# Fifteen gate blocks moved among the recurrent chain of a decoder block

## The chip, the cores and the metric

One core of one Trainium2 chip runs the whole program. The metric is device time in microseconds. Before the change it is 2598.03 us, the median of three runs (2596.94 to 2599.16).

## The reference, cut to what matters

One layer, one sequence of 512 tokens, width 1024, all float32. A modulation (shift, scale, gate) is computed from a conditioning vector; then:

```
h = rms_norm(x, norm1_gain) * (1 + scale1) + shift1
proj = h @ w_in     # aq ak av | dq dk dv | dz | dbeta dalpha | gate_a gate_b
y_a = sliding_window_attention(qa, ka, va, sinks) @ w_attn_branch
od  = gated_delta_rule(q, k, v, g, beta)          # 8 heads, chunks of 64 tokens
    # t_mat = inverse(eye + a_low); u = t_mat @ v_beta; w = t_mat @ (k_beta * exp(gc))
    # per chunk: v_new = u - w @ state
    #            o = (q * exp(g)) @ state + qk @ v_new
    #            state = state * exp(g_last) + (k * exp(g_last - g))^T @ v_new
od  = rms_norm(od, dn_out_norm) * silu(dz)
y_b = od @ w_dn_branch
mix = (sigmoid(gate_a) * y_a + sigmoid(gate_b) * y_b) @ w_out
x   = x + gate1 * mix
x   = x + gate2 * peer(rms_norm(x, norm2_gain) * (1 + scale2) + shift2, ...)
```

The last line, a mixer over 16384 experts, takes most of the time and is not touched.

## The kernel before, in words

Activations stand transposed: channels on the 128 partitions, tokens along the row. A float32 product with weights is made of three products of rounded halves: each weight slab and each activation is split into a high part (ScalarE rounds) and a low part (VectorE subtracts), and TensorE adds high by high, high by low and low by high. A block is 128 output channels by 512 tokens, 8 chunks of the contraction by 3 products, 24 matmuls of 512 columns. Slabs of two blocks (1 MB) come through the class `Stream`: SyncE loads, `split_hi` on ScalarE, `split_lo` on VectorE, `multiply` on TensorE, with two buffers. A load waits until the low part of the slab before last is made, a high split until the products of the slab before last are done.

Each phase is a block in which every engine has its own program, written out by hand in order. Engines wait for one another by counted semaphores; nothing reorders within an engine, so whatever is queued behind a waiting instruction waits too.

`phase_project` (L428) makes the projections for attention and for the delta rule, with the short convolution on VectorE (`conv`), and lets the attention's steps run among the delta rule's blocks. `ada_after` and `ada_mixed` say behind which block or in which attention step each of 32 chunks of the modulation is summed on TensorE; GpSimd makes the partial sums. `amplitude` (L838) is a chain of 36 small operations on VectorE, `decays` makes g, `sums` (L855) its running sum.

`phase_delta` (L912) is the recurrent stage. It takes four tiles of 128 tokens (two chunks), all 8 heads at once, two groups of four heads (`q`). For each tile: GpSimd copies this tile's k, v and coefficients to fixed places and writes the identity to `inv` and `invT`; ScalarE squares q and k; 32 instructions with a column of ones sum the squares (L992); the coefficients `cf` come from a root and an exponential; TensorE transposes k and v (L1002) and spreads coefficients over partitions (L1008, `spread`); ScalarE scales the transposed k and v (L1106 to L1108, 24 instructions); VectorE forms differences, scaled keys and queries, the decay `E`, and `AT` and `QKT`. The inverse is built in six levels (L1042, L1050, L1051, VectorE L1163, L1196, L1198). Then u and w (L1058, L1059), and for each chunk: w by state (L1072), difference `vnew` (L1210), state product (L1077), output (L1084 and L1085, states by scaled queries and values by scores, turn by turn in one bank), and the states' update on VectorE (L1216), which waits for the output as well. A hardware loop runs tiles 1 to 3. Nothing else uses TensorE in this stage, and the first two slabs of the mixing are loaded during the last tile.

`phase_mix` (L1237) streams 32 slabs: 4 for z (SiLU), then gate A and attention branch in turn (4 and 4), gate B and delta branch in turn (4 and 4), 4 for the output projection, 8 for the queries of the last mixer. `heads(s)` says which heads of the delta rule's output are normed behind slab s: two behind none and one each behind slabs 2 to 9; a head costs an all-ones matmul, a root on ScalarE, and a mean, a reciprocal and two products on VectorE.

## Time and profile before

| | us |
|---|---|
| median of three runs | 2598.03 |
| the profiled execution | 2598.93 |
| its span, first to last instruction | 2597.1 |
| TensorE busy | 2386.9 (92%) |
| VectorE busy | 1749.8 (67%) |
| ScalarE busy | 949.2 (37%) |
| GpSimd busy | 732.8 (28%) |
| mean granted clock of TensorE | 0.944 of full |

The profile's engines are PE (TensorE's matmuls), PEld (its weight loads, beside them), DVE (VectorE), ACT (ScalarE), POOL (GpSimd) and SP (SyncE). A matmul's busy time overlaps its neighbours', so TensorE's rate is read from the distance between starts. PEclk is the clock granted to TensorE as a share of 2.4 GHz; it has two levels, 0.50 and 1.00, and a figure between them is a mean over a stretch.

### The profile page before, as it was taken

How to read it: one execution, taken by the hardware profiler on the slowest of the kernel's cores; microseconds unless marked ns; L12 is line 12 of the kernel's file. 1: busy time of each engine (PE TensorE's matmuls, PEld its weight loads, DVE VectorE, ACT ScalarE, POOL GpSimd, SP SyncE). 2: the span in 40 equal slices, each digit the busy share in tenths (PEclk: the TensorE clock that was granted, in tenths of full speed). 3: DMA queues.
4: the chain of work that ended last, by engine and by line, in shares of the span. 5: the costliest groups of instructions: out<-in, count | busy, mean ns of one | idle time of the engine just before them, and what ended most of it. 6: DMA issues, size and time to landing. Idle time of an engine off the chain costs nothing.

```text
span 2597.1 us, 33865 instructions
## 1 busy us (share of the span) xinstructions
PE 2386.9 (92%) x13069; PEld 2078.5 (80%) x13069; DVE 1749.8 (67%) x3202; ACT 949.2 (37%) x1632; POOL 732.8 (28%) x661
## 2 busy tenths in 40 slices
PE   7898896887778899989899999989999999999998
PEld 2686776877777778768799999988888888888887
DVE  3469883342534374352698899978788887888877
ACT  2335783021120443232455555533333333333332
POOL 0467551010010000000366643343333333333330
PEclk9998997776968899999999999999999999999999
DMA  7333310000001232322333346699989888889984
GB/s 260 107 106 122 114 58 1 1 1 1 0 0 32 81 98 91 120 65 81 118 123 123 128 161 200 213 348 329 316 317 320 313 322 315 324 320 342 324 309 148
DMA packets 214691, 438.39 MB, mean 169 GB/s; under 512 B 22119, under 2 KB 129808, under 8 KB 214288
## 3 DMA queue, kind: packets, MB, share of 16 engines
q1 hardware_dynamic: 166752, 266.52, 30.5%
q0 software_dynamic: 45568, 163.60, 17.5%
q10 hardware_dynamic: 2224, 6.29, 0.6%
q8 instruction: 95, 1.56, 0.2%
q14 instruction: 52, 0.43, 0.0%
HBM read 392.32 MB, written 44.04 MB: 168 GB/s over the span
## 4 chain that ended last, share of the span: by engine, by line
PE 42%; DVE 8%; ACT 1%; issue 1%; DMA 0%; POOL 0%; ACTq 0%; POOLq 0%
PE bank L1823 20%; PE bank L1721 5%; DVE hot_j L2039 5%; PE bank L1809 3%; PE bank L1807 3%; PE bank L1808 3%; PE bank L1727 2%; PE bank L1691 2%; DVE hot_i L2034 2%; ACT ha L1871 1%; PE bank L1701 1%; PE bank L1743 1%; DVE o_nat L2103 0%; DMA ug<-in_peer_u_dram,gidx 0%; DVE o_nat L2102 0%
## 5 line engine op out<-in xcount | busy, mean ns | idle before, releaser
L1653 POOL TENSOR_TENSOR ua_lo<-ua,ua_hi 128x512 fp32r<-128x512 f32 x128 | 202.1, 1584 | 560.4 <-ACT ua L1858 560.2
L1823 PE MATMUL bank<-vt_hi,wg_hi 128*128 128x512 f32 x768 | 248.1, 404 | 5.2 <-DVE wg_lo L2093 4.9
L1646 POOL DMA_INDIRECT ug<-in_peer_u_dram,gidx x128 | 146.1, 1141 | 329.3 <-DVE ug L2049 326.3
L1823 PE MATMUL bank<-vt_lo,wg_hi 128*128 128x512 f32 x768 | 239.0, 392 | 0.0
L1823 PE MATMUL bank<-vt_hi,wg_lo 128*128 128x512 f32 x768 | 238.3, 391 | 0.0
L2075 DVE TENSOR_TENSOR vt_lo<-vt_raw,vt_hi 128x1024 fp32r<-128x1024 f32 x128 | 156.1, 1219 | 92.4 <-ACT vt_hi L1945 92.4
L1675 POOL DMA_INDIRECT vg<-in_peer_v_dram,gidx x128 | 131.2, 1025 | 237.9 <-DVE g_acc L2064 225.6
L1721 PE MATMUL bank<-h_hi,ua_hi 128*128 128x384 f32 x512 | 184.1, 360 | 12.3 <-ACT ha L1871 12.1
L1807 PE MATMUL bank<-h_hi,uT_hi 128*128 128x384 f32 x512 | 176.7, 345 | 0.0
L1721 PE MATMUL bank<-h_lo,ua_hi 128*128 128x384 f32 x512 | 174.0, 340 | 0.0
L1809 PE MATMUL bank<-h_hi,uT_lo 128*128 128x384 f32 x512 | 171.8, 335 | 0.0
L1823 PEld LDWEIGHTS bank<-vt_hi,wg_hi 128*128 128x128 f32 x768 | 135.3, 189 | 45.2 <-issue 24.3
L1945 ACT ACTIVATE vt_hi<-vt_raw 128x1024 fp32r<-128x1024 f32 x128 | 135.1, 1056 | 98.6 <-PE bank L1823 98.6
L1808 PE MATMUL bank<-h_lo,uT_hi 128*128 128x384 f32 x512 | 171.1, 334 | 0.0
L1823 PEld LDWEIGHTS bank<-vt_hi,wg_lo 128*128 128x128 f32 x768 | 144.8, 188 | 31.9
L1823 PEld LDWEIGHTS bank<-vt_lo,wg_hi 128*128 128x128 f32 x768 | 144.7, 188 | 31.8
L1956 ACT ACTIVATE wg_hi<-wt 128x384 fp32r<-128x384 f32 x128 | 67.3, 526 | 276.2 <-DVE wt L2088 273.0
L388 DVE TENSOR_TENSOR mx_lo<-mx_raw,mx_hi 128x2048 fp32r<-128x2048 f32 x32 | 73.3, 2292 | 137.1 <-ACT mx_hi L384 137.1
L2064 DVE SCALAR_TENSOR_TENSOR g_acc<-vg,g_hw,g_acc 128x1024 f32<-128x1024 f32 x127 | 162.5, 1280 | 1.4 <-DMA vg<-in_peer_v_dram,gidx 0.3
L2049 DVE SCALAR_TENSOR_TENSOR ug<-ug,h2n 128x1024 f32<-128x1024 f32 x128 | 155.5, 1217 | 3.2 <-DMA ug<-in_peer_u_dram,gidx 3.2
L2039 DVE TENSOR_SCALAR hot_j<-iota,picked,picked 128x128 f32<-128x128 f32 x384 | 145.7, 439 | 0.0
L1847 ACT ACTIVATE uT_hi<-bank 128x512 fp32r<-128x512 f32 x128 | 76.1, 594 | 189.5 <-PE bank L1691 189.5
(417 smaller groups left out, 5945.4 us busy)
## 6 DMA issues: line engine op xcount, KB each, us to landing
u_raw<-in_peer_u_dram SPq DMA_DIRECT2D x128, 512.0 KB
vt_raw<-in_peer_v_dram SPq DMA_DIRECT2D x128, 512.0 KB
gates<-g_stage SPq DMA_DIRECT2D x12, 2048.0 KB, 8.9
gate<-gates SPq DMA_DIRECT2D x32, 768.0 KB, 7.5
pj_raw<-in_w_in_dram SPq DMA_DIRECT2D x16, 1024.0 KB, 5.2
ada_w<-in_w_ada_dram POOLq DMA_DIRECT2D x32, 512.0 KB, 4.5
mx_raw<-in_w_in_dram SPq DMA_DIRECT2D x12, 1024.0 KB, 5.2
hid_keep<-ha POOLq DMA_DIRECT2D x64, 192.0 KB, 2.7
```

Source lines behind the costliest of these rows:

```text
L1646: nc.gpsimd.indirect_dma_start(ug[s % RING][:], None, u_rows, bass.IndirectOffsetOnAxis(m.gidx[:, s:s + 1].bitcast(U32), 0)).then_inc(s_ug ...
L1653: nc.gpsimd.tensor_tensor(ua_lo[b % 2][:, 4 * q:4 * q + 4, :], ua[b % 2][:, 4 * q:4 * q + 4, :], ua_hi[b % 2][:, 4 * q:4 * q + 4, :].bitca ...
L1721: last = pe.matmul(o, ua_hi[b % 2][:, k, :], (m.h2_lo if low else m.h2_hi)[:, k, P:], start=(n == 0), stop=False)
L1807: pe.matmul(o, uT_hi[f % 2][:, k, :], m.h2_hi[:, k, P:], start=(k == 0), stop=False)
L1808: pe.matmul(o, uT_hi[f % 2][:, k, :], m.h2_lo[:, k, P:], start=False, stop=False)
L1809: last = pe.matmul(o, uT_lo[f % 2][:, k, :], m.h2_hi[:, k, P:], start=False, stop=(k == KC - 1))
L1823: ins = pe.matmul(y_bank[t][q][:], w[n % 2][:, tok], v[n % 2][:, 512 * q:512 * q + 512], start=(first and i == 0), stop=(last and i == 2))
L1945: nc.scalar.activation(v_hi[n % 2][:], v_raw[n % 4][:], ACT.Copy).then_inc(x["vhi"], 1)
L2039: ins = v.tensor_scalar(B[n % 4][:, t, :], m.iota[:], jT[:, col], gT[:, col], ALU.is_equal, ALU.mult)
L2049: v.scalar_tensor_tensor(ug[s % RING][:], ug[s % RING][:], 1.0, m.h2n[:], ALU.mult, ALU.mult, accum_out=h_raw[:, s:s + 1]).then_inc(x["dot ...
L2064: ins = v.scalar_tensor_tensor(acc[:], vg[s % RING][:], h_w[:, s:s + 1], acc[:], ALU.mult, ALU.add)
L2075: v.tensor_tensor(v_lo[n % 2][:], v_raw[n % 4][:], v_hi[n % 2][:].bitcast(F32), ALU.subtract)\
```

## The change

Recurrent stage. The hardware loop is written out, so tiles are addressed directly, GpSimd's copies go, and so does the start value of the inverse. Fifteen blocks, the 8 of z and 7 of gate A, are computed in this stage: `load` on SyncE, `high` and `gate` on ScalarE, `low` on VectorE, and `fill(n)` on TensorE, which issues the next n of 360 matmuls at written places, with a pair of banks of their own. The gates of A go to DRAM tile by tile (`keep`) and are read back by the mixing. The weights of block 16 are split here as well. The first level of the inverse no longer multiplies by the identity: TensorE transposes `AT`, and VectorE masks both `AT` (with the new constant `above`) and its transpose. Values are scaled on VectorE (8 instructions), keys on ScalarE (16). The squares of the next tile wait only for the last `vnew`. States by scaled queries stand before the state product, values by scores come once for both chunks, behind everything, and the states' update no longer waits for the output.

Mixing. The order is: block 16 (the last of gate A), one gate slab of B, four of the attention branch, three gate slabs of B, four of the delta branch, then as before; 24 slabs instead of 32. Heads are normed behind slabs 0 to 5 as 1, 1, 2, 1, 1, 2.

Projection. Small moves of order, in the diff's first part.

```diff
-    ada_after = {i: [c] for c, i in enumerate((6, 8, 9, 10, 11, 12, 14, 15, 16, 17, 18, 19, 20))}
+    ada_after = {i: [c] for c, i in enumerate((6, 8, 9, 10, 12, 13, 18, 19, 20))}
@@ project, PE and DVE
-                if b == 1:        # transposes of g; on DVE sums()
+                if b == 2:
@@ project, ACT
+                if s == 0:
+                    split(2)
                 for half in range(2):
                     copy_out(2 * s + half)
-                split(s + 2)
+                if s:
+                    split(s + 2)
@@ and square(2), square(3) ahead of v_hi; on DVE amplitude() behind split_lo(5)
...
@@ delta, PE
+            def fill(n):
+                for i in range(place[0], place[0] + n):
+                    f, j = divmod(i, 3 * KC)
+                    k, term = divmod(j, 3)
+                    if j == 0:
+                        pe.wait_ge(f_lo, f + 1)
+                        if f >= 2:
+                            pe.wait_ge(f_read, f - 1)
+                    last = pe.matmul(F_BANK[f % 2][:], (hi, hi, lo)[term][f % 2][:, k, :],
+                                     (m.h_hi, m.h_lo, m.h_hi)[term][:, k, :], start=(j == 0), stop=(j == 3 * KC - 1))
+                    if j == 3 * KC - 1:
+                        last.then_inc(f_ready, 1)
+                place[0] += n
@@ fills in a tile, in order of the program
+                if not first:
+                    fill(24)                       # ahead of the ones-matmuls
+                fill(36 if first else 12)          # behind the spread of g
+                fill(0 if last_tile else 4)        # between the two score products
+                    if l < 4:                      # in each level, behind its first product
+                        fill(16 if l == 0 else 0 if last_tile else 3)
+                fill(8 if last_tile else 10)       # behind u and w
+                    fill(6)                        # in each chunk, ahead of the state product
+                    if c == 0:
+                        fill(0 if last_tile else 9)
@@ delta, PE, chunk
+                    for h in range(DNH):
+                        at = P * (h % G) + CHUNK * c
+                        pe.matmul(bank[h // G][:, at:at + CHUNK], S[:, h, :], qg[:, h, rows],
+                                  start=(c == 0 and h % G == 0), stop=False)
+                for h in range(DNH):               # once a tile, behind the second chunk
+                    last = pe.matmul(bank[h // G][:, P * (h % G):P * (h % G) + P], vnew[:, h, :], E[:, h, :],
+                                     start=False, stop=(h % G == G - 1))
@@ delta, ACT
+            def high(f):
+                act.wait_ge(f_loaded[f % 2], 16 * (f // 2 + 1))
+                if f >= 2:
+                    act.wait_ge(f_ready, f - 1)
+                nc.scalar.activation(hi[f % 2][:], raw[f % 2][:], ACT.Copy).then_inc(f_hi, 1)
@@ ACT per tile: squares, copies out of the tile before, gate(b0-1), high(b0+1), root, exp, scaled keys,
@@   exp of the differences, gate(b0), high(b0+2), gate(b0+1), high(b0+3), u and w, gate(b0+2), high(b0+4)
@@ DVE per tile: low(b0+1) first, low(b0+2) behind E, low(b0+3) behind the levels, low(b0+4) behind the
@@   first update of the states; in the first tile low(0) and low(1) behind the differences
@@ delta, DVE
+                    if l == 0:
+                        dve.wait_ge(z["Pm"], t * 12 + 2)
+                        for q in range(2):
+                            hs = slice(G * q, G * q + G)
+                            v.tensor_tensor(inv[:, hs, :], eye, prod[:, hs, :], ALU.subtract)
+                            v.tensor_tensor(invT[:, hs, :], eye, invT[:, hs, :], ALU.subtract).then_inc(z["D"], 1)
+                        continue
-                    dve.wait_ge(z["o"], t * 2 + (cc + 1))
@@ mix
-    A, B, OUT, WQ, N = 4, 12, 20, 24, 32
+    GATES, A, B, OUT, WQ, N = (0, 5, 6, 7), 1, 8, 12, 16, 24
-        return range(max(s - 2, 0), min(s - 1, DNH)) if s < B else range(0)
+        return ((0,), (1,), (2, 3), (4,), (5,), (6, 7))[s] if s < 6 else ()
+            for k in range(KC):
+                pe.matmul(bank[6][:], m.rest_hi[:, k, :], m.h_hi[:, k, :], start=(k == 0), stop=False)
+                pe.matmul(bank[6][:], m.rest_hi[:, k, :], m.h_lo[:, k, :], start=False, stop=False)
+                last = pe.matmul(bank[6][:], m.rest_lo[:, k, :], m.h_hi[:, k, :], start=False, stop=(k == KC - 1))
...
```

## Rows read from the trace of the kernel before

**Rows 1.** Stages: us; busy us (instructions) of PE, PEld, DVE, ACT, POOL; clock; DMA.
```profile
91.40:408.20 316.80, 279.44 (x1576) 229.57 (x1576) 238.83 (x356) 185.67 (x355) 187.09 (x167) 0.95 0.33 104
408.20:852.80 444.60, 354.62 (x2328) 340.65 (x2328) 170.62 (x366) 63.24 (x160) 28.08 (x33) 0.77 0.02 5
852.80:1084.90 232.10, 227.74 (x976) 185.07 (x976) 119.34 (x98) 87.78 (x94) 0.00 (x0) 0.98 0.28 91
```
**Rows 2.** Waits of the recurrent stage: who for whom: us in total, times, longest.
```profile
PE bank L992 <- ACT dn_sq L1096: 21.3, 4, 7.7
PE bank L1008 <- ACT vb L1108: 18.0, 4, 4.8
...
DVE states L1216 <- PE bank L1085: 78.3, 8, 11.0
```
**Rows 3.** Timeline (start, us), second chunk of tile 0: output and update.
```profile
513.93 0.69 PE L1084 MATMUL bank<-qg,states 128*128 128x64 f32 x2
...
521.13 2.15 DVE L1216 SCALAR_TENSOR_TENSOR states<-states,ee,bank 128x128 f32<-128x128 f32 x8 [10.96 <-PE bank L1085]
```
**Rows 4.** Short stretches: output matmuls of tile 0, transposes and scaled copies of tile 2.
```profile
494.00:500.00 6.00, 6.00 (x29) 5.78 (x29) 0.00 (x0) 0.00 (x0) 0.00 (x0) 0.50 0.00 0
647.00:648.00 1.00, 1.00 (x8) 1.00 (x8) 0.49 (x4) 0.00 (x0) 0.00 (x0) 0.68 0.00 0
650.00:654.00 4.00, 0.00 (x0) 0.00 (x0) 1.90 (x8) 4.00 (x17) 0.00 (x0) 1.00 0.00 0
```
**Rows 5.** Timeline, heads of tiles 1 and 2.
```profile
525.57 6.99 PE L992 MATMUL bank<-ones,dn_sq 128*128 128x1 f32 x32 [4.55 <-ACT dn_sq L1096]
534.07 0.17 DVE L1142 TENSOR_SCALAR dn_ms<-bank 128x16 f32<-128x16 f32 x1 [10.79 <-PE bank L997]
...
636.28 6.99 PE L992 MATMUL bank<-ones,dn_sq 128*128 128x1 f32 x32 [4.54 <-ACT dn_sq L1096]
646.15 1.77 PE L1002 MATMUL bank<-ident,vTs 128*128 128x128 f32 x8
```
**Rows 6.** Timeline, tile 0: first products of levels 0, 1 and 5, and u.
```profile
444.49 1.13 PE L1042 MATMUL bank<-inv,AT 128*128 128x128 f32 x8 [1.60 <-DVE AT L1163]
...
452.32 1.06 PE L1042 MATMUL bank<-inv,AT 128*128 128x128 f32 x8
...
476.75 1.06 PE L1042 MATMUL bank<-inv,AT 128*128 128x128 f32 x8
...
481.23 0.45 PE L1058 MATMUL bank<-vb,invT 128*128 128x128 f32 x2
```
**Rows 7.** Timeline of ScalarE, mixing: the first three blocks of z read.
```profile
865.48 0.60 ACT L1335 ACTIVATE z<-bank 128x512 f32<-128x512 f32 x1 [6.60 <-PE bank L423]
870.92 0.60 ACT L1335 ACTIVATE z<-bank 128x512 f32<-128x512 f32 x1 [4.84 <-PE bank L423]
...
876.36 0.60 ACT L1335 ACTIVATE z<-bank 128x512 f32<-128x512 f32 x1 [2.00 <-PE bank L423]
```
**Rows 8.** Timeline of TensorE, the first matmul of the mixing.
```profile
857.12 0.80 PE L421 MATMUL bank<-h_hi,mx_hi 128*128 128x512 f32 x1 [6.86 <-DVE mx_lo L388]
```
**Rows 9.** Timeline of VectorE, mixing: one head, from its mean to its last product.
```profile
920.89 0.68 DVE L1387 TENSOR_SCALAR od_rs<-bank 128x512 f32<-128x512 f32 x1
...
926.45 0.69 DVE L1394 TENSOR_TENSOR z<-od_rs,dn 128x512 f32<-128x512 f32 x1
```
**Rows 10.** Groups of the recurrent stage: count, busy us, mean ns, idle before.
```profile
L1177 DVE SCALAR_TENSOR_TENSOR E<-diff,dn_r,cum 128x128 f32<-128x128 f32 x32 | 12.8, 470 | 0.0
L979 POOL TENSOR_TENSOR Es<-E,strict 128x512 f32<-128x512 f32 x8 | 10.3, 1288 | 117.0 <-DVE E L1177 117.0
```
**Rows 11.** Waits of TensorE in the projection.
```profile
PE bank L655 <- DVE g L835: 9.1, 1, 9.1
...
PE bank L562 <- DVE pj_lo L388: 3.5, 1, 3.5
PE bank L582 <- ACT at_sq L682: 3.2, 1, 3.2
```

More of the change, by code:

```diff
@@ L125, in constants @@
     m.level = m.small("level", [P, 6, P])
+    m.above = m.small("above", [P, P])
     m.amask = m.small("amask", [P, 2, 2 * P])
@@ L992, in body @@
                     pe.matmul(bank[0][:, j:j + 1], sq[:, j, :], m.ones[:, 0:1], start=True, stop=True)
-                pe.wait_ge(z["stage"], t * 2 + 1)
-                pe.matmul(bank[0][:, 24:32], sel[:], gs[:], start=True, stop=True)
+                pe.matmul(bank[0][:, 24:32], sel[:], gs, start=True, stop=True)
                 for c in range(2):
@@ L1020, in body @@
                         pe.wait_ge(z["kb"], t * 2 + (h // G + 1))
-                    last = pe.matmul(bank[2 + h // G][:, P * (h % G):P * (h % G) + P], kTs[:, h, :], kb[:, h, :],
+                    last = pe.matmul(bank[2 + h // G][:, P * (h % G):P * (h % G) + P], kT[:, h, :], kb[:, h, :],
                                      start=True, stop=True)
@@ L1079, in body @@
                     last.then_inc(z["st"], 1)
-                    if c == 1:
-                        pe.wait_ge(z["oe"], t * 2 + 1)
-                    for h in range(DNH):
-                        cols = slice(CHUNK * h, CHUNK * h + CHUNK)
-                        pe.matmul(bank[4][:, cols], S[:, h, :], qg[:, h, rows], start=True, stop=False)
-                        last = pe.matmul(bank[4][:, cols], vnew[:, h, :], QKT[:, h, rows], start=False, stop=True)
-                    last.then_inc(z["o"], 1)
+                    if c == 0:
+                        fill(0 if last_tile else 9)
@@ new lines, in gate @@
+            def gate(f):
+                act.wait_ge(f_ready, f + 1)
+                if f < DNH:
+                    nc.scalar.activation(m.z[:, f, :], F_BANK[f % 2][:], ACT.Silu).then_inc(f_read, 1)
+                else:
+                    if f > DNH:
+                        act.wait_ge(f_sig, 16 * (f - DNH))
+                    nc.scalar.activation(sig[:], F_BANK[f % 2][:], ACT.Sigmoid).then_inc(f_read, 1)
+            for t in range(NT):
+                tok = slice(P * t, P * t + P)
+                b0 = 4 * t
+                if t:
+                    act.wait_ge(z["vn"], t * 2)
+                nc.scalar.activation(sq[:, DNH:, :], m.dn[:, DNH:2 * DNH, tok], ACT.Square)
+                nc.scalar.activation(sq[:, 0:DNH, :], m.dn[:, 0:DNH, tok], ACT.Square).then_inc(z["sq"], 1)
+                if t:
+                    act.wait_ge(z["o"], t)
+                    nc.scalar.activation(m.carry[:], m.ones[:, 0:1], ACT.Copy)
+                    for q in range(2):
+                        last = nc.scalar.activation(m.dn[:, G * q:G * q + G, P * (t - 1):P * t],
+                                                    bank[q][:].rearrange("p (h n) -> p h n", h=G), ACT.Copy)
+                    last.then_inc(z["oe"], 1)
+                    gate(b0 - 1)
+                    high(b0 + 1)
@@ L1173, in body @@
                     by(q, qg, m.dn[:, G * q:G * q + G, tok], 6, z["qg"])
+                dve.wait_ge(z["bq1"], t + 1)
+                for q in range(2):
+                    by(q, q1, m.dn[:, G * q:G * q + G, tok], 0, z["q1"])
                 for q in range(2):
@@ L1218, in body @@
                     last.then_inc(z["S"], 1)
-            loop(dve, body, c, 4)
+                    if cc == 0 and t < NT - 1:
+                        low(b0 + 4)
 def mix_slabs(a):
@@ L1228, in mix_slabs @@
     w_q = a["peer_w_q"].rearrange("o (k p) n -> p (o k) n", p=P)
-    slabs = [w_in[:, :, COL_Z + SLAB * i:COL_Z + SLAB * i + SLAB] for i in range(DNW // SLAB)]
-    for gate, branch in (((w_in, COL_GA), (w_a, 0)), ((w_in, COL_GB), (w_b, 0))):
-        for i in range(D // SLAB):
-            slabs += [w[:, :, base + SLAB * i:base + SLAB * i + SLAB] for w, base in (gate, branch)]
+    part = lambda w, base: [w[:, :, base + SLAB * i:base + SLAB * i + SLAB] for i in range(D // SLAB)]
+    gates = part(w_in, COL_GB)
+    slabs = gates[:1] + part(w_a, 0) + gates[1:] + part(w_b, 0)
     slabs += [w_o[:, :, SLAB * i:SLAB * i + SLAB] for i in range(D // SLAB)]
@@ L1328, in _ @@
             split(1)
+            for k in range(KC):
+                nc.scalar.activation(y_hi[:, k, :], at[:, k, :], ACT.Copy).then_inc(z["ahi"], 1)
+            act.wait_ge(z["rest"], 1)
+            nc.scalar.activation(sig_a[3][:, 1, :], bank[6][:], ACT.Sigmoid).then_inc(z["rest_sig"], 1)
             square(0)
@@ L1331, in _ @@
             for s in range(OUT):
-                if s < A:
-                    for half in range(2):
-                        act.wait_ge(st.ready, 2 * s + half + 1)
-                        nc.scalar.activation(m.z[:, 2 * s + half, :], bank[2 * (s % 2) + half][:], ACT.Silu)\
-                            .then_inc(st.read, 1)
-                elif s % 2 == 0:
-                    gate(s, sig_a if s < B else sig_b)
+                if s in GATES:
+                    gate(s)
                 if s == OUT - 1:
@@ L1420, in _ @@
                         low_mix(k)
-                if s > A and s % 2:
+                if s not in GATES:
                     branch(s)
-                if s == B:
+                if s + 2 < OUT + 1:
+                    st.split_lo(dve, s % 2, s + 2)
+                for n in heads(s):
+                    mean(n)
+                    normed(n)
+                if s == 6:
                     for k in range(KC):
```

303 lines of the change are left out of this document (169 added, 134 removed).

## The prediction

> **What bounds the kernel now.** The stage table comes first [rows 1]: projection 316.8 us, the recurrent stage (delta rule) 444.6 us, the mixing up to the output projection 232.1 us, the rest 1512 us. Only the first three change. TensorE is busy in 279 of 317, 355 of 445 and 228 of 232 us, but in the recurrent stage its granted clock averages 0.77 against 0.95 and 0.98 beside it. So the mixing is bound by TensorE's work alone, and the recurrent stage by a chain of engines that hand on to each other, with half-clock matmuls in it. The waits of the stage say the same from both sides [rows 2]: TensorE waits 21.3 us for the squares at the head of each tile and 18.0 us for ScalarE's scaled copies, VectorE 78.3 us for the last output matmul before it may update the states. The timeline shows that last one: the state product is out at about 513.9, then the output's 32 instructions run until 521.1, and only then comes the update of 2.15 us, though it needs the state product alone [rows 3]. The clock rows tell what is slow in there: 0.50 in the output matmuls [rows 4], and the ones-matmuls take the time of that clock too (below). A tile's period, from ones to ones, is 636.28 - 525.57 = 110.7 us [rows 5].
>
> **Units.** An fp32 matmul is two instructions here. One level of the inverse is 48 instructions in (476.75 - 452.32) / 4 = 6.11 us [rows 6], a wait of some 0.7 among them; they follow each other every 0.111 us at full clock. The 32 ones-matmuls and six more take from 525.57 to 534.07, less a little latency 8.2 us at half clock [rows 5], 0.217 each, so 0.107 to 0.111 at full clock. A gate block (24 matmuls of 512 columns) takes 876.36 - 870.92 = 5.44 us [rows 7], 0.227 each.
>
> **Mixing: what is removed.** 20 slabs of two blocks stand before the output projection; 12 and one single block are left. Eight slabs by 10.88 us are 87.0 us gone. The single block comes first. Today TensorE waits 6.9 us there and starts at 857.12, 4.3 us into the stage [rows 8]; the new block needs no split and fills that hole, but runs mostly at half clock as the first matmuls do now (the first half is read at 865.5, 8.3 us for 24 matmuls). It ends about 8.0 us in; the first block ended its cold part (2.9 us above 5.44) and the 4.3 us start before, so 0.8 us is lost net. Heads: one costs VectorE 926.45 + 0.69 - 920.89 = 6.2 us, a low split 2.2 [rows 9], two products of a branch 1.4. I lay them out in the new order (heads 1, 1, 2, 1, 1, 2 behind slabs 0 to 5; blocks of 5.44, a head's own squares on TensorE 0.9). VectorE is through with head 1 at 41 us, 3 at 59, 4 at 69, 5 at 79, 7 at 96, and the eight low parts of y at 103; slabs 3, 5 and 6 find their weights split within 0 us of need, and TensorE comes to the first delta branch slab (8) at 102.4. So a stall of 0.6. Mixing gain: 87.0 - 0.8 - 0.6 = 85.6 us. Its bounds: the 79 us that remain if the new single block is fully exposed and the heads stall 1.5 us, and 87.
>
> **Recurrent stage, a middle tile at full clock.** Zero is the end of the second chunk's state matmuls. TensorE: values by scores for all heads in 16 instructions 1.8; fill of 24, 5.4 (to 7.2); ones and sums 4.1 (11.3). Beside it the update of the states (2.2), ScalarE's two copies out, a gate (0.6, a table load of 1.3 with it) and a split (1.1) end by 7.6, and the squares were made before, since they now wait for nothing but the chunk's difference; so the 21.3 us wait goes. Coefficients 2.8 us later as now, 14.1; 16 transposes and 16 spread instructions to 14.9; fill 12 to 17.6. ScalarE's scaled copies are 16 now instead of 24, a quarter us each (17 in 4.0 us): 4.0 plus latency, 18.5. VectorE takes the other eight (2.1) and the differences (some 2.2), 18.5 as well [rows 4]. TensorE stalls 0.9 instead of 4.5 [rows 2]. Three spreads (5.4), first product 1.8, fill 4 of 0.9, second 1.8: 28.4. VectorE: last scaled query 25.3, E 3.2 (28.5, 0.4 us pitch from [rows 10]), GpSimd's mask 1.3 (29.8), AT at 30.4 and 31.0. The first level now is 8 transposes, 16 fills hidden behind VectorE's two score products, two masks, two products and four differences of about 0.6 each: 31.0 + 5.3 = 36.3. From its first product to the next level's that is 5.9 us where it is 452.32 - 444.49 = 7.8 now [rows 6], so only 2 us go. Levels 1 to 3 take 6.1 + 0.7 for three fills (a fill between product and product is added, since the wait of 0.48 behind it stays) less 0.4 at the first, level 4 6.1, the last with the two products behind it 8.1 (481.23 - 476.75 and 3.6) [rows 6]: 70.2. ScalarE's copies 2.1, under ten fills: 72.5. Each chunk is 16 + 16 + 6 fills + 16 instructions, 1.8 + 1.8 + 1.4 + 1.8 = 6.8, with VectorE's difference (1.3) under the fills, and 2.4 for the update between them, under nine fills: 72.5 + 6.8 + 2.4 + 6.8 = **88.5 us**, against 110.7.
>
> Where the cover could go: the splits of VectorE (1.2 each) stand in front of the coefficients, behind E, behind the last level and behind the update. Each is done 1 to 4 us before what TensorE wants next; if one is late it costs its own 1.2. SP's eighteen steps (loads of 512 KB, keeps of 256 KB behind them) always wait for an event of an earlier group; a keep has some 10 us before its tile is written again.
>
> **First and last tile.** At the first, the squares start at 408.3 and not 411.4, ones end 418.6 (half clock), G at 424.4. Then TensorE must wait for VectorE's eight copies, the differences and two splits: 427.9. 36 fills take 8.2 and about 2.5 for a cold start: 438.6; from there as above (88.5 - 18.5): 508.6, where it is 513.9 now. The last tile has 24 fills fewer, but only those on the chain count (3 x 0.7): 86.5. Then 3.2 for the last output and copies. Stage: 100.4 + 177.0 + 86.5 + 3.2 = 367.1 against 444.6, so 77.5 us gone at full clock.
>
> **Clock.** Ones-matmuls, chunk matmuls of 64 rows or columns: these ran at 0.50 [rows 4, 5]. Now warm fills stand between them. Bounds: nothing, and all of it at half clock, that is 6.8 x 2 + 2.0 + 1.8 + 5.4 + 4.1 + 3.6 = 30.5 us more per tile, four times 122, less some 14 of stalls that it covers, 108. I take 3 us for the head of each of three tiles (one drop in the ones, paid in the transposes) and 1 us per recurrence, 13 us, near the lower end, because of all rows at half clock none has 512-column matmuls close before it. Stage gain: 64.5 us.
>
> A rule that speaks against this: between 647 and 648 the clock rises to full (0.68 in the mean), and what runs there is the second half of the transposes, from 646.15 on [rows 4, 5]. The Trainium skill (TensorE: Matmul & The Clock Gate, Part 4: PE-mode transpose) says that full clock doesn't engage for transpose-mode matmuls. By that rule 24 transposes per tile would be paid at 0.217 instead of 0.111, 10 us over four tiles; by the row nothing. I go by the row.
>
> **Projection.** Three waits [rows 11]. The 3.5 us one: VectorE's 36 small operations (7.2 us) stood before the split of slab 2; moved away, TensorE no longer waits there, but the split now precedes the copy out, and the wait for that copy of 1.0 grows by 1.9: net -1.8 (it starts at 94.1, ends 99.7, before 101.5). The moved operations fall into VectorE's idle 8.9 us. The 3.2 us for the squares shrinks by v_hi's 2.0. The 9.1 us for g: one more block (5.4) goes in front, but the next needs a bank that the first convolution frees, so 2.4; the scans then stand later on VectorE, by up to 2.7 for the first softmax. Four more modulation chunks go among the attention steps: GpSimd needs 5.8 us for one, a step lasts 11.5, hidden. Sum -5, between -8 and -1. The constant `above` costs three operations of 0.25 us under the loads.
>
> **Sum.** The profiled execution lasted 2598.93 us (span 2597.1), 0.9 over the median of 2598.03. 2598.9 - 85.6 - 64.5 - 5 = 2443.8; the median may be 0.9 lower. I forecast **2444 us**.
>
> **Rivals.**
> - No clock loss: 13 us less, 2431. For it: a TensorE almost without gaps. Against: the 38 ones and sums in a row. 0.13.
> - The clock stays half in head and recurrence (the 108 instead of 13): 2539. For it: all rows of these matmuls at 0.50. Against: 60 fills in those stretches. 0.10.
> - Heads late: if each of eight roots needs its table load (1.3) on VectorE's path, slab 8 waits 10 us: 2454. Now it is loaded ahead in all rows. 0.12.
> - The transposes go unclocked, the rule above: 2454, 0.04.
> - The fills cost in the recurrent stage what the edits there save: stage at 444 as now, only 85.6 + 5 gained, 2508. 0.05.
> - Slower: the fills run neither warm nor hidden. 360 matmuls at 0.453 are 163 us in line; the other edits of the stage give back about 57 (three operations of the first level 21, GpSimd's copies 9, 128 output instructions 27). Stage +106, others -91: 2614. It decides from a growth of the stage by 91 us. Against: TensorE was idle 90 us there. 0.02.
> - The projection gains nothing: 2449, 0.04.
> - Forecast, 2430 to 2458: 0.50.
>
> The range 2422 to 2480 leaves out the three far cases (0.17). About 0.2% (5 us) can be told from no change. Faster 0.975, same 0.005, slower 0.02.
>
> **What would show it.** The stage table: recurrent stage about 380 us at a clock of 0.95 or more, mixing 146 to 147 until the output projection, projection 312. TensorE's wait for the squares gone, the one for the scaled copies about 1 us a tile, VectorE's 78.3 us gone, period 89 to 94. Wrong if the period is over 98, if ones or chunk matmuls show 0.50 over whole tiles, if TensorE waits in the fills for a low split, or if slab 8 of the mixing waits for over 3 us.

## The result, and the profile after

The changed kernel takes 2448.14 us (median of 4 runs, 2446.27 to 2452.55) where the kernel before takes 2597.61 (2596.94 to 2599.16): 0.9425 of its time, 95% interval 0.9411 to 0.944. The forecast was 2444. The profiled span is 2444.4 us against 2597.1. The stage table, cut at the same events as before (start and end; us; busy us and instructions of PE, PEld, DVE, ACT, POOL; granted clock; DMA share; GB/s):

```profile
91.00:409.30 318.30, 280.89 (x1576) 230.17 (x1576) 252.31 (x355) 185.59 (x355) 189.14 (x166) 0.94 0.33 103
409.30:789.20 379.90, 350.24 (x2464) 320.40 (x2464) 200.02 (x418) 82.63 (x159) 14.80 (x9) 0.94 0.11 33
789.20:933.40 144.20, 143.52 (x616) 115.48 (x616) 100.80 (x89) 55.20 (x64) 0.00 (x0) 1.00 0.31 101
```

Beside [rows 1]: the recurrent stage went from 444.6 to 379.9 us (-64.7; forecast -64.5), the mixing from 232.1 to 144.2 (-87.9; forecast -85.6), and the projection ends 1.1 us later (it starts 0.4 earlier, so it is 1.5 longer) where -5 was forecast. What follows takes 1511.0 us instead of 1512.2. The four together are -152.7, the whole difference of the spans. In the recurrent stage TensorE issues 136 instructions more (360 of the gates, minus those removed), and the granted clock is 0.94 instead of 0.77.

The waits of that stage (who for whom: us in total, times, longest):

```profile
DVE states L1315 <- PE bank L1115: 32.0, 8, 4.0
PE bank L1071 <- DVE AT L1250: 10.5, 8, 2.7
...
PE bank L1019 <- ACT dn_sq L1152: 4.5, 1, 4.5
```

The wait for the squares, 21.3 us at four tiles in [rows 2], is left at the first tile alone (4.5); the 18.0 us for the scaled copies are gone altogether; VectorE waits 32.0 us for the state product instead of 78.3 for the output. What each of these is worth alone isn't shown: the experiments take back only the update's place (e6) and the first level (e3). The timeline of tile 2 shows what stands there now (start, us, instructions):

```profile
603.52 2.05 PE L1121 MATMUL bank<-E,vnew 128*128 128x128 f32 x16
603.62 2.15 DVE L1315 SCALAR_TENSOR_TENSOR states<-states,ee,bank 128x128 f32<-128x128 f32 x8 [3.99 <-PE bank L1115]
610.89 4.86 PE L1019 MATMUL bank<-ones,dn_sq 128*128 128x1 f32 x32
616.90 3.38 PE L1028 MATMUL bank<-ident,dn 128*128 128x128 f32 x16
636.55 0.66 PE L1071 MATMUL bank<-ident,AT 128*128 128x128 f32 x4 [1.75 <-DVE AT L1250]
643.01 2.27 PE L1073 MATMUL bank<-inv,AT 128*128 128x128 f32 x16 [0.81 <-DVE invT L1292]
```

The update starts with the output product (603.62 beside 603.52) and no longer behind the output's 32 instructions, as it did in [rows 3]. From one output product to the next are 92.85 us here; the four stand at 512.15, 603.52, 696.37 and 785.68. Two stretches of the same tile show the clock, chunks and then ones and transposes:

```profile
589.00:603.00 14.00, 14.00 (x97) 11.91 (x97) 5.64 (x13) 2.01 (x2) 0.00 (x0) 1.00 0.15 39
613.00:619.00 6.00, 6.00 (x30) 6.00 (x30) 0.68 (x5) 1.68 (x3) 0.00 (x0) 0.50 0.01 3
```

In the mixing TensorE starts at full clock and waits once, before the first delta-branch slab:

```profile
789.24 0.47 PE L1387 MATMUL bank<-h_hi,fl_hi 128*128 128x512 f32 x1 [1.51 <-PEq L953]
889.78 0.50 PE L426 MATMUL bank<-y_hi,mx_hi 128*128 128x512 f32 x1 [0.64 <-DVE y_lo L1542]
```

The waits of TensorE in the projection have changed names and not their sum:

```profile
PE bank L608 <- DVE sd L804: 15.8, 4, 10.9
PE bank L619 <- ACT sc L707: 14.5, 11, 4.3
PE bank L567 <- ACT kn L680: 2.9, 1, 2.9
PE bank L587 <- ACT at_sq L687: 1.3, 1, 1.3
```

### The profile page after: what moved, and what is told of

Same layout as the page of the kernel before. It is cut to its first block, busy times and chain, and to the rows that moved or that the text cites. A ratio compares the mean times of both kernels' runs of the same rounds, so it can differ in the third digit from the quotient of the medians.

```text
span 2444.4 us, 33257 instructions
## 1 busy us (share of the span) xinstructions
PE 2299.5 (94%) x12845; PEld 1989.1 (81%) x12845; DVE 1774.4 (73%) x3248; ACT 935.5 (38%) x1601; POOL 723.1 (30%) x637
## 4 chain that ended last, share of the span: by engine, by line
PE 45%; DVE 8%; ACT 2%; issue 1%; POOL 0%; ACTq 0%; DVEq 0%
PE bank L1929 22%; PE bank L1827 5%; DVE hot_j L2145 5%; PE bank L1915 4%; PE bank L1913 4%; PE bank L1914 4%; PE bank L1833 3%; PE bank L1797 2%; DVE hot_i L2140 2%; ACT ha L1977 1%; PE bank L1807 1%; PE bank L1849 1%; DVE o_nat L2209 0%; DVE o_nat L2208 0%; PE bank L1897 0%
## 5 line engine op out<-in xcount | busy, mean ns | idle before, releaser
L2181 DVE TENSOR_TENSOR vt_lo<-vt_raw,vt_hi 128x1024 fp32r<-128x1024 f32 x128 | 156.5, 1223 | 92.5 <-ACT vt_hi L2051 92.5
L2150 DVE TENSOR_TENSOR uT_lo<-bank,uT_hi 128x512 fp32r<-128x512 f32 x128 | 88.3, 690 | 81.9 <-ACT uT_hi L1953 81.9
```

What stands on the lines that cost most here:

```text
L2181: v.tensor_tensor(v_lo[n % 2][:], v_raw[n % 4][:], v_hi[n % 2][:].bitcast(F32), ALU.subtract)\
```

## The experiments

All are edits of the changed kernel. "Against it" is the ratio less 0.9425, times 2598 us; an interval of a ratio is 3 to 6.5 us to either side, that of the changed kernel 3.7. The intervals of e6, e7, e8, e10 and e11 lie apart from the changed kernel's; those of e1, e2, e3, e4, e5, e9 and e12 touch or overlap it, and what is said of these rests on their traces.

| run | median us (range) | ratio [95%] | against it, us |
|---|---|---|---|
| e1 bare fills | 2441.68 (2440.44 to 2444.28) | 0.9396 [0.9379, 0.9414] | -7.5 |
| e2 chunks bare | 2454.97 (2454.54 to 2457.16) | 0.9449 [0.9431, 0.9466] | +6.2 |
| e3 level 0 by products | 2459.09 (2454.5 to 2464.28) | 0.9458 [0.9433, 0.9483] | +8.6 |
| e4 projection undone | 2447.52 (2442.66 to 2450.3) | 0.9421 [0.9408, 0.9434] | -1.0 |
| e5 modulation undone | 2444.71 (2443.07 to 2448.0) | 0.9415 [0.9402, 0.9428] | -2.6 |
| e6 output ahead of update | 2462.71 (2461.98 to 2467.3) | 0.9482 [0.9463, 0.9501] | +14.8 |
| e7 heads late | 2464.83 (2462.67 to 2469.4) | 0.9492 [0.9477, 0.9506] | +17.4 |
| e8 fills redealt | 2433.71 (2433.21 to 2434.48) | 0.9371 [0.9357, 0.9385] | -14.0 |
| e9 scans behind softmax | 2446.18 (2443.01 to 2450.25) | 0.9419 [0.9406, 0.9432] | -1.6 |
| e10 = e8 + e5 | 2431.86 (2428.56 to 2437.03) | 0.9363 [0.935, 0.9375] | -16.1 |
| e11 = e10 + e9 | 2426.80 (2421.76 to 2431.42) | 0.9346 [0.9333, 0.9358] | -20.5 |
| e12 sums early | 2442.22 (2437.74 to 2446.84) | 0.9401 [0.9388, 0.9414] | -6.2 |

**What the fills cost (e1).** Of each gate block only the first and the last matmul are issued.

```diff
+                    if 0 < j < 3 * KC - 1:
+                        continue
                     last = pe.matmul(F_BANK[f % 2][:], ...
```

> The changed kernel, with 22 of the 24 matmuls of each of the fifteen moved blocks left out (330 of 360, 75 us of TensorE at full clock); the loads, splits, gates and waits stay. Theory (the fills lie mostly under other engines' work and hold the clock at 1.00): at full clock a middle tile would lose only the exposed fills, some 8 of 22 us, but the ones-matmuls and the chunk matmuls fall back to 0.50 and cost about 18 us a tile more; the recurrent stage stays near 380 us (370 to 400), the kernel within -10 to +20 us of the changed one. Rival (the fills are a load on TensorE's path, the clock doesn't depend on them): the stage loses 30 to 75 us and the kernel with it, clock still over 0.9.

330 matmuls of 0.227 us, 75 us of TensorE's work, are gone, and 7.5 us with them. Timeline of TensorE, the second chunk of tile 1 and the head behind it:

```profile
586.08 3.67 PE L1107 MATMUL bank<-states,wT 128*64 128x128 f32 x16 [2.25 <-DVE states L1317]
589.68 3.68 PE L1112 MATMUL bank<-qg,states 128*128 128x64 f32 x16
...
593.82 3.78 PE L1117 MATMUL bank<-vnew,kdec 64*128 64x128 f32 x16
597.53 3.78 PE L1123 MATMUL bank<-E,vnew 128*128 128x128 f32 x16
...
602.63 4.72 PE L1021 MATMUL bank<-ones,dn_sq 128*128 128x1 f32 x32 [0.63 <-issue]
```

Sixteen instructions take 3.7 us and not 2.0: half clock, which with the fills was full. The four groups cost 7 us more, and idle stretches of 1.7 to 3.2 us come back elsewhere, as the first row shows one. The periods, output product to output product, are 91.4, 92.2 and 92.2 us beside 91.4, 92.85 and 89.3 with the fills. So in the middle tiles the 20 us of 88 fills are paid by two things. From 597.53 to 689.70 in e1 TensorE is busy 76.7 of 92.2 us at a mean clock of 0.83; from 603.52 to 696.37 in the changed kernel 87.7 of 92.85 us, at 0.96. Its busy time fell by 11 us where 20 of work are gone, so some 9 are the clock that the fills hold, and idle time grew by 10. The theory's bounds for stage and kernel held, its terms less well: it had put the clock at 18 us a tile. What is left is in the first tile: 89.9 us from its ones (416.27) to its last output product (506.14), where it is 100.6 with the fills.

**Where the fills stand (e2, e8).** e2 takes all fills out of levels 1 to 3 and the chunks and puts them in front of the chunks (24 for 10) and into the first level (32 for 16). e8 keeps three in each chunk, takes those between the products of levels 1 to 3 away, puts eight where TensorE waits for AT, behind the score products, and the others behind the spread of g (4 more), into the first level (6 more) and behind the first state product (1 more). Its diff, without the last tile's counts:

```diff
-                fill(36 if first else 12)
+                fill(40 if first else 16)
...
+                fill(8)
-                fill(0 if last_tile else 4)
...
-                        fill(16 if l == 0 else 0 if last_tile else 3)
+                        fill((18 if last_tile else 22) if l == 0 else 0)
...
-                    fill(6)
+                    fill(0 if last_tile else 3)
```

> The changed kernel with the same 360 fills, but none among the two chunks of a tile and none in levels 1 to 3: they stand behind the first product of level 0 (32) and behind u and w (24). Theory (fills among the chunk matmuls keep the clock up there): the chunk matmuls show 0.50 again, some 5 to 11 us a tile, the kernel is 20 to 45 us slower than the changed one. Rival (what precedes is warm enough, the place is indifferent): the chunks stay at 1.00 and only the balance of exposed fills changes, 0 to +6 us.

> The changed kernel with its 360 fills dealt otherwise: in a middle tile 24 ahead of the ones, 16 behind the spread of g, 8 behind the second score product, 22 in level 0, none in levels 1 to 3, 10 behind u and w, 3 in each chunk, 10 behind the first state product. Theory (a fill is free where TensorE waits and costs 0.227 us elsewhere; some 17 fills a tile move from exposed to covered places): -2 to -4.5 us a tile, the kernel 8 to 17 us faster, clock as now. Rival (three fills a chunk are too few to hold the clock): the chunks show 0.50, 10 us or more slower.

e2, TensorE at the second chunk of tile 1 and the first level of tile 2:

```profile
602.60 3.14 PE L1105 MATMUL bank<-states,wT 128*64 128x128 f32 x16 [2.25 <-DVE states L1312]
605.67 2.43 PE L1110 MATMUL bank<-qg,states 128*128 128x64 f32 x16
...
642.92 0.66 PE L1071 MATMUL bank<-ident,AT 128*128 128x128 f32 x4 [1.75 <-DVE AT L1247]
...
653.56 1.95 PE L1073 MATMUL bank<-inv,AT 128*128 128x128 f32 x16
```

The chunks lost 1.6 us to the clock (3.14 + 2.43 for 1.96 + 2.00) and took 15.5 us in all where they took 16.8 with fills; with the 24 fills ahead of them the clock needed few inside. The time went into the first level, where 32 fills make 10.6 us of 6.5, and into the stretch ahead of the chunks. The balance of tile 2, from output product to output product (96.4 us beside 92.85), is +4.2 there, -2.3 in the other levels, +3.2 ahead of the chunks and -1.4 in the chunks. The 6.2 us lie by the rival's 0 to 6; the theory, a loss of clock in the chunks, asked 20 to 45 and falls. But the chunks didn't stay at 1.00, as the rival had it: they ran at 0.89 in the mean. e8 turns that reading round:

```profile
602.07 2.05 PE L1121 MATMUL bank<-E,vnew 128*128 128x128 f32 x16
634.25 0.66 PE L1071 MATMUL bank<-ident,AT 128*128 128x128 f32 x4 [0.83 <-DVE AT L1250]
641.10 1.95 PE L1073 MATMUL bank<-inv,AT 128*128 128x128 f32 x16
```

Periods fall to 90.6, 88.9 and 84.2 us, and from the first ones to the rest block it is 365.4 us instead of 377.6. Of the 4.0 us of the tile shown, 2.3 are levels 1 to 5, mostly the fills between products (0.7 a level, as that step of the prediction had it), 1.2 the chunks (15.6 us for 16.8), and 0.8 the way to AT (32.2 us for 33.0). The first level became 0.4 longer. The way to AT holds eight fills more (1.8 us) and is shorter all the same: TensorE waits 0.83 us for AT and not 1.75, and the ones run at full clock (3.63 us for 4.86). The theory's 8 to 17 holds.

**The first level (e3).** Products with a staged identity instead of transposes and masks.

```diff
-                                last = pe.transpose(o, AT[:, h, :], m.ident[:])
+                            last = pe.matmul(o, AT[:, h, :], inv[:, h, :], start=True, stop=True)
```

> The changed kernel with the first level of the inverse as before: identity written by GpSimd at the tile's start, product with it, two products more. Theory (this level is VectorE's chain plus TensorE's 48 instructions, and the fills stand in it): 3.3 us a tile later, +8 to +14 us for the kernel. Rival (the level is hidden behind the 16 fills and the differences of VectorE): within 2.5 us of the changed kernel.

```profile
644.21 2.38 PE L1074 MATMUL bank<-inv,AT 128*128 128x128 f32 x16 [1.82 <-DVE AT L1250]
...
653.66 1.06 PE L1074 MATMUL bank<-inv,AT 128*128 128x128 f32 x8
```

9.45 us from first product to next level, 6.46 with the masks: 3.0 a tile, 12 in four, and +8.6 by the ratio, 11 by the medians. As the theory had it; the rival, a hidden level, falls by the trace. The four runs are two pairs, 2454.5 and 2455.2, 2463.0 and 2464.3. The trace is of the slower pair, and from the first ones to the rest block it takes 394.1 us instead of 377.6, 4.5 more than the level explains.

**Output ahead of the update (e6).** Each chunk's share of the output is computed behind its state product, in front of what VectorE waits for.

```diff
                     last.then_inc(z["st"], 1)
+                    for h in range(DNH):
+                        last = pe.matmul(bank[h // G][:, at:at + CHUNK], vnew[rows, h, :], E[rows, h, rows], ...
+                    last.then_inc(z["o"], 1)
...
                     dve.wait_ge(z["st"], t * 2 + (cc + 1))
+                    dve.wait_ge(z["o"], t * 2 + (cc + 1))
```

> The changed kernel with the output's second product once per chunk (64 columns, 64 rows) straight behind the state product, and the states' update waiting for it, as before the change. Theory (the order costs its 16 instructions at full clock in the first chunk; in the second the fill of 24 covers it): +1.8 us a tile, +5 to +9 us. Rival (these narrow matmuls pull the clock down, which is what cost 7 us a chunk before): the clock falls below 0.9 in the chunks and the kernel is 20 us or more slower.

VectorE's wait and the start of the rest block:

```profile
DVE states L1317 <- PE bank L1120: 46.9, 8, 6.1
```
```profile
803.58 0.76 PE L1389 MATMUL bank<-h_hi,fl_hi 128*128 128x512 f32 x1 [2.59 <-PEq L953]
```

The wait grew from 32.0 to 46.9 us, 1.9 for each of eight chunks, and the rest block starts 14.3 us later than the 789.24 of the changed kernel. It also starts at half clock (0.76 us for its first matmul), which it doesn't there. The 14.8 us lie between the theory's 5 to 9 and the rival's 20; the share of the first chunk alone, 1.9 a tile in TensorE's own order, would be 8. The trace shows most of the other half. In tiles 1 and 2 it is 12.8 us from the first chunk's start to the second's, where the changed kernel takes 9.6: 1.9 for the 16 instructions, and 1.3 since most of the nine fills behind them run at half clock:

```profile
696.20 0.63 PE L1002 MATMUL bank<-h_lo,fl_hi 128*128 128x512 f32 x1
...
699.23 1.96 PE L1105 MATMUL bank<-states,wT 128*64 128x128 f32 x16
```

The nine take 3.6 us from 695.61 and not 2.3, at a clock of 0.66 between 693.6 and 698.4. That is the rival's mechanism, at 1.3 us a tile and not at the 7 a chunk that it named. In the first and the last tile this distance is 11.4 us; in the last the clock falls in the second chunk instead (0.81 from 790 to 799).

**Heads (e7).** One head behind each of the slabs 0 to 7, as in the kernel before.

```diff
-            return ((0,), (1,), (2, 3), (4,), (5,), (6, 7))[s] if s < 6 else ()
+            return (s,) if s < 8 else ()
```

> The changed kernel with one head normed behind each of slabs 0 to 7 of the mixing instead of 1, 1, 2, 1, 1, 2 behind slabs 0 to 5, and the split of the normed heads behind slab 7. Theory (the first delta branch slab then waits for the last head and eight splits on VectorE): TensorE waits about 15 us ahead of slab 8, +11 to +17 us. Rival (the heads are hidden anyway): within 2.5 us.

```profile
904.38 0.80 PE L426 MATMUL bank<-y_hi,mx_hi 128*128 128x512 f32 x1 [14.93 <-DVE y_lo L1542]
```

14.9 us of wait instead of 0.64, and a clock of 0.62 from 904 to 912. The head's place is worth what the layout of the order said.

**The projection (e4, e5, e9, e12).** e4 puts all its edits back; e5 only the groups of the modulation on GpSimd; e12 only the place of the sums; e9 leaves that place and moves the scans behind the first softmax.

In e4 and e5, ahead of the modulation's chunks; in e4 and e12, at the transposes and at the sums:

```diff
-    ada_after = {i: [c] for c, i in enumerate((6, 8, 9, 10, 12, 13, 18, 19, 20))}
+    ada_after = {i: [c] for c, i in enumerate((6, 8, 9, 10, 11, 12, 14, 15, 16, 17, 18, 19, 20))}
...
-                if b == 2:
+                if b == 1:
```

In e4 alone, also the order of v's high part and of the squares, and the place of VectorE's 36 small operations; in e9 alone the last two lines:

```diff
-                if s == 0:
-                    split(2)
                 for half in range(2):
                     copy_out(2 * s + half)
-                if s:
-                    split(s + 2)
+                split(s + 2)
...
             st.split_lo(dve, 1, 5)
-            amplitude()
...
                     soft(at_score[b])
+                if b == 2:
+                    scans()
```

> The changed kernel with every edit of the projection undone (modulation chunks, transposes of g, order of split and copy, squares, amplitude). Theory from the two traces (the stage ends 1.1 us later after the change, 409.3 against 408.2): the edits bring nothing, the kernel is 0 to 3 us faster than the changed one. Rival (my forecast): they bring 5 us, the kernel is 1 to 8 us slower.

> The changed kernel with only the modulation chunks dealt as before (13 ahead of the attention, 19 in its steps). Theory (GpSimd's work and VectorE's small operations stretch one another: g ends 14 us earlier while GpSimd waits, but four chunks more among the attention steps slow VectorE, which bounds there): g takes 14 us again as before, the attention steps are faster, together within -6 to +2 us of the changed kernel. Rival (GpSimd is indifferent): VectorE's operations keep their times and the kernel its time within 2 us.

> The changed kernel with one thing moved: the two scans and the addition over the decays (5.3 us of VectorE in the trace of the changed kernel, 204.5 to 209.8, ahead of the first softmax) are issued behind the first softmax instead of ahead of it; the copy out of PSUM stays ahead. In the changed kernel TensorE waits 10.9 us at 213.1 for that softmax. Theory (the first softmax is on the path and VectorE has room later): that wait falls from 10.9 to about 5.6, and 3 to 5 us of it reach the end: 2443 to 2445. Rival (from 200 us on VectorE's own queue, busy 46 of 50 us, sets the pace, so the order of its work is of no account): the wait falls but the next ones grow by as much, 2447 to 2449, no change. Worse than 2450 would say that the transposes of the decays now hold TensorE up.

> The changed kernel with one thing undone: the transposes of the decays and their sums stand again behind the second block of the mixed-layer projection and not behind the third. Theory of the prediction (that move took 2.4 us off the path): 2450 to 2451. Rival (the wait for the decays had been over anyway, since they are ready at 188 us in the changed kernel and no longer at 202, so the place is of no account): 2447 to 2449. If the later place is what put the sums ahead of the first softmax, the undone version is faster: 2443 to 2446.

VectorE in the changed kernel, ahead of the first softmax (its last step at 212.92 releases TensorE's `scores` at 213.14, the 10.9 us wait):

```profile
203.81 0.67 DVE L866 COPY gT<-bank 8x512 f32<-8x512 f32 x1
204.52 3.08 DVE L868 TENSOR_TENSOR_SCAN run<-keep,gT 8x512 f32<-8x512 f32 x1
207.63 1.10 DVE L869 TENSOR_TENSOR_SCAN off<-keep,run 8x32 f32<-8x32 f32 x1
208.77 1.10 DVE L872 TENSOR_TENSOR run<-run,off 8x384 f32<-8x384 f32 x1
209.80 1.64 DVE L798 SCALAR_TENSOR_TENSOR sc<-bank,qrs,amask 128x256 f32<-128x256 f32 x4
```

With the sums one block earlier, e12: VectorE, and TensorE's first `scores` and first ones-matmul.

```profile
190.72 0.67 DVE L866 COPY gT<-bank 8x512 f32<-8x512 f32 x1
191.43 1.21 DVE L868 TENSOR_TENSOR_SCAN run<-keep,gT 8x512 f32<-8x512 f32 x1
...
193.48 2.27 DVE L393 TENSOR_TENSOR pj_lo<-pj_raw,pj_hi 128x2048 fp32r<-128x2048 f32 x1
...
198.68 1.65 DVE L798 SCALAR_TENSOR_TENSOR sc<-bank,qrs,amask 128x256 f32<-128x256 f32 x4
```
```profile
203.65 2.08 PE L608 MATMUL bank<-kn,aq 64*128 64x256 f32 x8 [4.81 <-DVE sd L804]
...
400.26 6.96 PE L1019 MATMUL bank<-ones,dn_sq 128*128 128x1 f32 x32 [4.51 <-ACT dn_sq L1152]
```

The first softmax starts at 198.7 and not 209.8, and the ones at 400.26 and not 411.60: 11 us in this execution, of which its later stages gave 6 back (1661.5 us from the rest block on, instead of 1655.2), and 6 in the medians. The intervals of e12 and of the changed kernel still touch (0.9414 and 0.9411).

Not all of the 11 us are the edit's. The last v_hi products of a block that stands ahead of the moved instructions in both, in the changed kernel and in e12:

```profile
173.33 1.16 PE L578 MATMUL bank<-v_hi,h_hi 128*128 128x272 f32 x8
```
```profile
169.85 1.16 PE L578 MATMUL bank<-v_hi,h_hi 128*128 128x272 f32 x8
```

e12 is 3.5 us early there already, 0.4 from the start of the stage and 3.1 by the clock: between 165 and 175 us it was 1.00, in the changed kernel 0.59 and 0.73, with the same instructions in the same order. This drop, behind the squares of attention's q (`at_sq`), stands in the traces of e1, e2, e3, e6, e7, e8 and e9 too; e12's was spared it, so how much of the 6 us in the medians is the place isn't shown. The other 7.6 us lie between the first convolution and the first softmax, 21.6 us in the changed kernel (188.18 to 209.80) and 14.0 in e12. The sums stand in front of that softmax in both. In e12 VectorE makes them while GpSimd is idle, in 2.8 us with their copy and not 6.0 (3.2); they fill the 2.5 us that VectorE otherwise waits for ScalarE's high part of the slab; and the low part behind takes 2.27 us and not 4.10 (1.8):

```profile
196.78 4.10 DVE L393 TENSOR_TENSOR pj_lo<-pj_raw,pj_hi 128x2048 fp32r<-128x2048 f32 x1 [2.50 <-ACT pj_hi L675]
```

That the later place harms, the third reading in e12's expectation, is what fits; the prediction's gain of 2.4 from the move is out.

How far such a difference can be read: the changed kernel and those with its projection (e1, e2, e3, e6, e7, e8) start the ones between 411.6 and 416.3. So e4 (411.0) and e9 (410.5) can't be told from it by their traces, nor by their ratios, and e4's equal time says what the stage table says: the projection's edits brought nothing that can be measured. e5 (407.8) starts them 3.8 us early, of which 3.1 are there before g is made, nearly all by the same clock (1.00 from 165 to 175), as in e10 and e11, which deal the modulation as e5 does. Its mechanism is as its theory had it: g takes 14 us again beside a busy GpSimd, and TensorE waits 3.4 us for it. In e9 the wait for the softmax fell from 10.9 to 5.8, as the theory had it, and too little of it reached the end to be told from none. The scans moved behind bring the first softmax 5.3 us nearer to the first convolution (16.35 us), moved ahead 7.6; where the rest of the difference between e9 and e12 comes from, beyond the 3.1 us of clock, is open.

**Together (e10, e11).**

> The redealt kernel (2433.7) with the modulation groups among the projection's slabs as in the kernel before. Alone on the changed kernel that return brought 2448.1 to 2444.7, with ScalarE's and VectorE's small operations beside GpSimd's work at other places. Theory (the two add, since they act in different stages): 2430 to 2431. Rival (the 3.4 us were the phase in which the recurrent stage meets the clock, not the projection): 2433 to 2435 here.

> The redealt kernel with the modulation groups as before the change and the two scans behind the first softmax. Theory (all three add): 2425 to 2428. Rival (VectorE's queue sets the pace of the projection's second half): as the redealt kernel with the modulation groups alone, 2430 to 2434.

e10 can't be told from e8 (0.9363 and 0.9371, intervals overlapping). e11 is the fastest version measured, 2426.80 us, 0.9346 of the kernel before and outside the interval of the changed kernel; that it adds to e10 isn't certain (0.9363 [0.935, 0.9375]). e8 with the sums early was not run.

## Why the prediction was right, and where it was not

**Mixing, -85.6 forecast, -87.9 measured.** Eight slabs less, and a stall of 0.6 before slab 8: 0.64, with the place of the heads confirmed by e7. The term that was off is the single block: 8.0 us "mostly at half clock" against 5.5 at full clock (0.47 us for its first matmul, where [rows 8] has 0.80), and that is 2.5 us better than forecast. The stretch before it is one of dense work with an idle of 1.5 us; in [rows 8] TensorE had been idle for 6.9. e6, with 2.6 us idle, starts the block at half clock.

**Recurrent stage, -64.5 forecast, -64.7 measured.** First tile, from the stage's start to the output product: 100.4 plus 1 for the clock forecast, 102.9 measured (409.30 to 512.15). Middle tiles: 88.5 plus 4 for the clock, so 92.5; measured 91.4 and 92.85. Last tile: 86.5 plus 4; measured 89.3. The end, 3.2 forecast, is 3.5. So the stage's agreement to 0.2 us is partly luck: errors of up to 1.5 us cancel. The prediction's own terms up to the end of the levels add up to 70.5 and not to its 70.2. Inside a tile: ones at 7.2 forecast, 7.4 measured; the first transposes of AT at 30.4 plus 3 for the head's clock, measured 33.0; first level 5.9 forecast, 6.46 measured, since TensorE still waits 0.67 between its two halves and 0.8 at its end; chunks 16.0 forecast, 16.8 measured, at full clock, so the 1 us a recurrence put down to the clock wasn't lost to it, and the instructions took 0.8 more than their sum. The clock step held in kind: full in the chunks (1.00), and one drop in the ones, paid in the transposes (4.86 and 3.38 us for what takes 3.6 and 1.9 at full clock, 2.7 us). Half clock in the recurrence, the rival of 2539, is what e1 shows without fills, though only in part (0.84 from the first ones to the rest block, 0.95 with them): its stage isn't longer, since the fills' own time is gone with it. The rival in which the fills cost what the edits save falls with the stage's 64.7 us.

**The transposes.** In [rows 4, 5] the granted clock rose while transposes ran. In e4 all 16 transposes of k and v of a tile, one instruction each, ran at full clock, behind ones at full clock:

```profile
612.48 1.94 PE L1025 MATMUL bank<-ident,dn 128*128 128x128 f32 x16
```

0.11 us each. The rule of the Trainium skill (TensorE: Matmul & The Clock Gate, Part 4: PE-mode transpose) that full clock doesn't engage for them does not hold here; no loss of 10 us stands anywhere. The 1.4 us that they lost in the tile of the changed kernel shown above came with the clock that fell in the ones ahead of them.

**Projection, -5 forecast, +1.1 measured.** The failed step is "one more block (5.4) goes in front ... so 2.4; the scans then stand later on VectorE, by up to 2.7". The other waits went as forecast: 3.5 gone with kn's grown from 1.0 to 2.9, the squares' from 3.2 to 1.3. The wait for g went whole, since g is ready at 188.3 and not 202.2, but the sums then stand at 203.8 to 209.8, 6.0 us in front of the first softmax, and TensorE waits 10.9 us there instead of 9.1 for g. The place was priced at 2.7 us, which is what copy, scans and addition take in the kernel before (208.15 to 210.82), with GpSimd idle. In the changed kernel they take 6.0 beside GpSimd, the low part ahead of them 4.10 instead of 2.27, and VectorE idles 2.5 ahead of that: 7.6 us by the traces of e12 and the changed kernel. How much of it reaches the end isn't settled: 6.2 by e12's ratio, with touching intervals and 3.5 of the 11 us of its trace's lead there before the place is reached. The prediction counted GpSimd's work among the attention steps as "hidden", from GpSimd's own time alone, and put nothing on VectorE for it. That g would come 14 us early was missed too: with four modulation groups fewer among the slabs GpSimd is idle while VectorE works on g, and VectorE's small operations take their bare time (last section).

## What to carry to other kernels

Independent matmuls dealt into a dependent chain are paid for by idle time and by the clock that they hold; look in a trace for what each place waits, and deal no more there than that, since between one product and the product behind it every fill costs its own length (0.7 us for three, in e8). When a wait of the fast engine goes, look at what its releaser has queued in front of the next thing wanted, and beside which engine it will run: the 9 us wait for g went, and one of 11 for the first softmax came. Lay moved work out in order on the engine that carries it: for the heads, where this was done, the forecast wait was within 0.1 us of the measured one, and for the sums, where it wasn't, the forecast was several us off.

## What the runs showed of the hardware

A small operation of VectorE with two inputs in SBUF can take fourteen times its length beside GpSimd. The same polynomial step in the kernel before, with what GpSimd did, and in the changed kernel, with GpSimd idle from 183.4 to 195.1:

```profile
187.72 2.62 DVE L831 TENSOR_TENSOR g<-g,dn_t 128x32 f32<-128x32 f32 x1
190.37 1.31 DVE L832 TENSOR_SCALAR g<-g 128x32 f32<-128x32 f32 x1
```
```profile
187.42 0.92 POOL L512 DMA_DIRECT2D ada_w<-in_w_ada_dram  x1 [0.30 <-POOL ada_acc L527]
188.36 1.91 POOL L519 TENSOR_TENSOR ada_w<-ada_w,silu_c 128x1024 f32<-128x1024 f32 x1
190.35 2.14 POOL L523 TENSOR_TENSOR ada_w<-ada_w 128x512 f32<-128x512 f32 x2
```
```profile
184.52 0.19 DVE L839 TENSOR_TENSOR g<-g,dn_t 128x32 f32<-128x32 f32 x1
```

2.62 us and 0.19 for one form: the first ends at 190.34, just behind GpSimd's 1024-column product at 190.27, and the next, 1.31, ends about with the first of its two sums. The Trainium skill (SBUF — State Buffer, section SBUF: two separate sides) says that GpSimd and a VectorE operation with two inputs in SBUF share one port pair, which whoever starts first holds for the whole instruction. The trace agrees in the end of the wait, and the price is GpSimd's instruction and not VectorE's; but VectorE's operation is shown as begun at 187.72, 0.6 us ahead of that product, while GpSimd still issued a load, so who came first these rows don't show. The scan at 204.52 took 3.08 us in the changed kernel and 1.21 in the one before: it ended 1.1 us behind GpSimd's product of 204.60 to 206.51. The busy time of VectorE in the projection rose from 238.8 to 252.3 us with an operation fewer; that all of it comes from there isn't shown. Modulation groups moved away from one place made g early there (e5, which moves them back, has g at 195.9 again); beside GpSimd's work at the next, VectorE's operations were longer.
